# Attention scores two pairs ahead, zero matmuls at the changes of stage, and weight remainders split up, in a two-block network kernel

## The reference

```python
def sliding_window_attention(u, k, v, w_q, q_norm, sinks, rel_bias, w_o):
    q = rmsnorm((u @ w_q).reshape(...), q_norm)
    ...
    def block(args):                         # 128 queries against 256 keys
        s = einsum('bqkrd,bskd->bkrqs', qk, kk) * scale + bias
        s = where(valid, s, -inf)
        m = maximum(max(s), sink)
        p = exp(s - m)
        denom = sum(p) + exp(sink - m)
        return einsum('bkrqs,bskd->bqkrd', p / denom, vk)
    ...
    return o @ w_o
```

## Time and profile before

| | |
|---|---|
| median of 3 runs | 2444.01 us (2443.07 to 2445.93) |
| the profiled execution | 2443.57 us, its span 2441.5 us |
| mean granted clock of PE | 0.964 of full speed |
| busy: PE | 2213.6 us (91%) |
| busy: DVE, ACT | 1517.4 us (62%), 1005.7 us (41%) |
| weight transfers | 354.88 MB on SP's queue, 44.1% of 16 engines |

### The profile page before, as it was taken

The page is one execution under the profiler, slowest core; times in us unless marked ns, Lnnn a source line. Parts: engine busy times, 40 slices in busy tenths (PEclk is TensorE's granted clock), DMA queues, the critical chain, the costliest instruction groups (busy, mean ns, idle before and its releaser), DMA issues.

```text
span 2441.5 us, 43688 instructions
## 1 busy us (share of the span) xinstructions
PE 2213.6 (91%) x15328; PEld 1975.8 (81%) x15336; DVE 1517.4 (62%) x2937; ACT 1005.7 (41%) x1601; POOL 17.0 (1%) x23
## 2 busy tenths in 40 slices
PE   7998787999989987799898878997788999999998
PEld 6998786799979975699887647886766999999997
DVE  4555776655545544555575556888966666666665
ACT  4344453533443444533452244224533444444443
POOL 0000000000000000000000000000000000000000
PEclk9999898999989999899999989998999999999999
DMA  5554342455465543355440013433355766666664
GB/s 190 181 188 165 133 143 70 145 193 191 167 224 180 188 132 101 112 188 190 147 147 29 11 43 129 145 113 109 130 166 180 235 204 204 219 187 189 188 188 132
DMA packets 106677, 376.95 MB, mean 154 GB/s; under 512 B 11552, under 2 KB 17456, under 8 KB 105840
## 3 DMA queue, kind: packets, MB, share of 16 engines
q1 hardware_dynamic: 102528, 354.88, 44.1%
q0 software_dynamic: 4080, 21.15, 2.7%
HBM read 362.29 MB, written 13.69 MB: 154 GB/s over the span
## 4 chain that ended last, share of the span: by engine, by line
PE 77%; DVE 9%; DMA 4%; ACT 4%; issue 3%; DVEq 2%; ACTq 1%; SPq 0%
PE bank L340 60%; PE bank L366 6%; PE bank L1325 3%; DVE w_lo L301 2%; DMA ring<-in_expert_v 2%; PE bank L2188 1%; DMA ring<-in_ssm_in 1%; ACT w_hi L296 1%; DVE arena L2389 1%; DMA ring<-in_expert_u 1%; PE bank L531 1%; PE bank L322 1%; PE bank L768 1%; ACT arena L1123 1%; PE bank L324 1%
## 5 line engine op out<-in xcount | busy, mean ns | idle before, releaser
L301 DVE TENSOR_TENSOR w_lo<-ring,w_hi 128x1024 fp32r<-128x1024 f32 x581 | 701.7, 1223 | 459.1 <-ACT w_hi L296 457.8
L296 ACT ACTIVATE w_hi<-ring 128x1024 fp32r<-128x1024 f32 x581 | 604.4, 1056 | 694.6 <-PE bank L340 540.9
L340 PE MATMUL bank<-u_hi,w_hi 128*128 128x256 f32 x2568 | 733.6, 286 | 10.9 <-DVE arena L861 7.7
L340 PE MATMUL bank<-u_lo,w_hi 128*128 128x256 f32 x2568 | 730.2, 284 | 0.0
L340 PE MATMUL bank<-u_hi,w_lo 128*128 128x256 f32 x2568 | 729.8, 284 | 0.0
L340 PEld LDWEIGHTS bank<-u_hi,w_hi 128*128 128x128 f32 x2568 | 496.2, 193 | 22.2 <-issue 10.4
L340 PEld LDWEIGHTS bank<-u_lo,w_hi 128*128 128x128 f32 x2568 | 496.3, 193 | 7.5 <-issue 0.5
L340 PEld LDWEIGHTS bank<-u_hi,w_lo 128*128 128x128 f32 x2568 | 495.8, 193 | 0.0
L340 PE MATMUL bank<-w_hi,x_hi 128*128 128x512 f32 x992 | 396.0, 399 | 21.0 <-DVE w_lo L301 14.8
L340 PE MATMUL bank<-w_lo,x_hi 128*128 128x512 f32 x992 | 392.8, 396 | 0.0
L340 PE MATMUL bank<-w_hi,x_lo 128*128 128x512 f32 x992 | 389.6, 393 | 0.0
(11 more groups left out here) (304 smaller groups left out, 1789.4 us busy)
## 6 DMA issues: line engine op xcount, KB each, us to landing
ring<-in_w SPq DMA_DIRECT2D x264, 512.0 KB, 3.6
ring<-in_expert_u SPq DMA_DIRECT2D x128, 512.0 KB, 3.6
ring<-in_expert_v SPq DMA_DIRECT2D x128, 512.0 KB, 4.3
ring<-in_ssm_in SPq DMA_DIRECT2D x40, 512.0 KB, 4.3
gate_dram<-con SPq DMA_DIRECT2D x16, 576.0 KB, 3.0
arena<-gate_dram POOLq DMA_DIRECT2D x9, 1024.0 KB, 8.7
ring<-in_ssm_out SPq DMA_DIRECT2D x16, 512.0 KB, 3.4
ring<-in_w_o SPq DMA_DIRECT2D x16, 512.0 KB, 4.2
```

The costliest lines, as they stand in the source:

```text
L296: act.activation(w_hi[slot][:, :], ring[slot][:, :], ACT.Copy).then_inc(hi_made[slot], 1)
L301: dve.tensor_tensor(w_lo[slot][:, :], ring[slot][:, :], w_hi[slot][:, :].bitcast(F32), ALU.subtract).then_inc(freed[slot], 1)
L340: mm = pe.matmul(out, left[a], right[b], start=start and n == 0, stop=stop and n == 2, skip_group_check=True)
```

## The change

Three edits.

1. **Attention.** The banks are dealt by use and no more by parity: `Q` (banks 0, 1), scores `SC` (2, 3), transposes `PT` (4, 5), outputs `OUT` (6). In step j PE does the transposes of pair j, the query sums of j+2, the outputs of j, the queries of j+3 and the scores of j+2. ACT does the copies of j, the root of j+2, the output copy of j, the exponentials of j+1 and the squares of j+3. DVE takes the maxima of j+1, makes the queries of j+2 and scales the probabilities of j+1. SP's queue is put in the matching order.
2. **Zero matmuls.** `norm_tensor` issues eight matmuls of zeros (bf16, 512 columns, into bank 4) ahead of its first wait and four more between its two halves, in all changes of stage but those at the start and behind kv: ssm, ffn1, kv, attn, ffn3, rwkv and peer, 84 matmuls in all.
3. **Remainders.** Of a stage's led tiles the first remainder is made where all were, the second between `update_h` and `norm_vector`, and the rest behind `norm_vector`.

```diff
-        def lead_vector(dve, before):
-            after = stages[stages.index(before) + 1:][:1] if before else stages[:1]
-            for slot, ring_stage in LEAD.get(after[0], ()) if after else ():
+        def lead_vector(dve, stage, some):
+            for slot, ring_stage in LEAD.get(stage, [])[some]:
                 make_lo(dve, slot, ring_stage, 0)
+
+        def lead_next(dve, before):
+            for stage in stages[stages.index(before) + 1:][:1]:
+                lead_vector(dve, stage, slice(0, 1))
...
-            lead_vector(dve, stage)
+            lead_next(dve, stage)
             update_h(dve, 0.5, upd[stage], stage)
...
+        def keep_busy(pe, n):
+            for _ in range(n):
+                pe.matmul(bank[4][:, :], zeros[:, 0:P], zeros[:, :], start=True, stop=True)
+
         def norm_tensor(pe, s):
+            calm = s == stages[0] or stages[stages.index(s) - 1] == "kv"
+            if not calm:
+                keep_busy(pe, 8)
             for q in range(4):
+                if q == 2 and not calm:
+                    keep_busy(pe, 4)
                 pe.wait_ge(S("norm_rows"), 4 * norm_no[s] + q + 1)
...
+            query(0, 0)
+            query(1, 0)
+            table(0, 0)
+            query(0, 1)
+            table(1, 0)
+            with sp.Fori(0, 2) as i:
+                query(1, i + 1)
+                table(0, i + 1)
+                query(0, i + 2)
+                table(1, i + 1)
+            query(1, 3)
+            table(0, 3)
+            table(1, 3)
...
-            def step(b, i):
-                nb, ni = 1 - b, i + b
-                queries(nb, ni)
+            def step(b, i, further=True, ahead=True):
                 turn(b, i)
-                query_sums(nb, ni)
+                if ahead:
+                    query_sums(b, i + 1)
                 outputs(b, i)
-                scores(nb, ni)
+                if further:
+                    queries(1 - b, i + 1 + b)
+                if ahead:
+                    scores(b, i + 1)
...
+            def step(b, i, further=True, ahead=True, more=True):
+                j1 = 2 * i + b + 1
                 for a in range(2):
                     act.wait_ge(S("p_turned"), 2 * j1 - 1 + a)
-                    act.activation(prob_t[:, b, a, :], bank[4 * b + a][:, 0:384], ACT.Copy).then_inc(S("p_turned_out"), 1)
+                    act.activation(prob_t[:, b, a, :], PT[a][:, 0:384], ACT.Copy).then_inc(S("p_turned_out"), 1)
+                if ahead:
+                    root(b, i + 1)
+                act.wait_ge(S("o_done"), j1)
+                act.activation(o_all[:, bass.ds(2 * i + b, 1), :], OUT[:, 0:T].unsqueeze(1),
+                               ACT.Copy).then_inc(S("o_ready"), 1)
                 if more:
-                    root(nb, ni)
+                    exps(1 - b, i + b)
+                if further:
+                    square(1 - b, i + 1 + b)
...
+            def step(b, i, ahead=True):
+                maxima(1 - b, i + b)
+                if ahead:
+                    query(b, i + 1)
+                normalise(1 - b, i + b)
...
                 if s in norm_no:
+                    if s != stages[0]:
+                        lead_vector(dve, s, slice(1, 2))
                     norm_vector(dve, s)
-                    if s == stages[0]:
-                        lead_vector(dve, None)
+                    lead_vector(dve, s, slice(0 if s == stages[0] else 2, None))
```

More of the change, by code:

```diff
@@ L1033, in attn_sync, with query @@
             sp.wait_ge(S("h_updated"), 4 * upd["attn"] + 1)
-            with sp.Fori(0, 4) as i:
-                for b in range(2):
-                    load(sp, b, io["w_q"][bass.ds(2 * i + b, 1), :, :], "attn", i)
-                    sp.wait_ge(S("scored"), 4 * i + 2 * b + 2)
-                    for a in range(2):
-                        table = bias_dram[bass.ds(4 * i + 2 * b + a, 1), 127:127 + P * 383].rearrange(
-                            "h (q y) -> q (h y)", y=383)
-                        sp.dma_start(bias_tile[:, b, a, 0:P], table[:, P:2 * P]).then_inc(S(f"bias_loaded{b}"), 16)
-                        sp.dma_start(bias_tile[:, b, a, P:384], table[:, 0:2 * P]).then_inc(S(f"bias_loaded{b}"), 16)
+            def query(b, i):
+                load(sp, b, io["w_q"][bass.ds(2 * i + b, 1), :, :], "attn", i)
@@ L1151, in query, with maxima @@
                 dve.wait_ge(S("qk_rooted"), 2 * i + b + 2)
-                dve.scalar_tensor_tensor(q_t[:, b, :], bank[4 * b][:, 0:T], V("q_norm"), at_root[:, b, :],
+                dve.scalar_tensor_tensor(q_t[:, b, :], Q[b][:, 0:T], V("q_norm"), at_root[:, b, :],
                                          ALU.mult, ALU.mult).then_inc(S("q_ready"), 1)
-            def step(b, i, more=True):
+            def maxima(b, i):
                 j1 = 2 * i + b + 1
@@ L1193, in attn_vector @@
                 step(1, i)
-            step(0, 3)
-            step(1, 3, more=False)
+            step(0, 3, ahead=False)
             out_vector(dve, "attn_out", o_all)
```

90 lines of the change are left out of this document (53 added, 37 removed).

## The result

| | before | after |
|---|---|---|
| median | 2443.54 us (4 runs, 2442.26 to 2445.93) | 2417.22 us (4 runs, 2411.58 to 2423.82) |
| ratio, 95% interval | | 0.9895 (0.9877 to 0.9912) |
| profiled execution, its span | 2443.57, 2441.5 us | 2418.02, 2416.0 us |
| mean granted clock | 0.964 | 0.968 |

The forecast was 2420 (2413 to 2429), faster: it held. The kernel is 1.05% faster. Note how far apart the four runs after lie, 12 us.

A forecast was written before the change was run, and what follows sets the result against it. No engine is full: PE waits in serial chains or runs at half clock. Attention -21.1, ffn3 -2.7, ffn1 -1.2, rwkv -1.1 and ssm +3.0 sum to -23.1, from 2443.57 to 2420.5, said as 2420 us; range 2413 to 2429.

The forecast's parts named there:

- The loop: Attention loop: seven steps take 47.0 us against 71.0, five of 6.8 and two of 6.5; -24.0 us.
- the rings: Attention step: the longer of two serial rings sets it, DVE and ACT at 6.5 us, PE at 6.8.
- low clock inside the loop: Attention loop: sign of failure, as are steps staying above 8 us; no size given.
- ffn3 and ffn1: Changes of stage into them: products start 1.1 us earlier; ffn3 -2.7 with 1.6 of low clock gone, ffn1 -1.2.
- The ssm stall: ffn0 to ssm: PE stands 3.5 us for the dt remainder, then half clock; +3.0 us, bounds +1.7 and +5.6.
- rwkv: ffn3 to rwkv: next tiles wait for loads, so only the earlier u_lo counts; -1.1 us.
- The zero matmuls: Changes of stage: covered by PE's waits, cost taken as 0; full clock kept, eight transposes 1.10 us instead of 1.97.
- zeros don't hold the clock: Rival, changes of stage: 0.44 lost at three of them and 1.6 us in ffn3; 2423.4 us, chance 0.08.
- The queue: Rival, attention: w_q loads stuck behind bias tables on SP's queue land late; slower, 2456 us, chance 0.03.
- Long steps: Rival, attention: further semaphore waits on PE and late maxima make steps of 8.5 us; 2433 us, chance 0.09.
- The cheap stall: Rival, ssm: stall costs +0 to +1.7 instead of +3.0, each attention step 6.5 us; 2417 us, chance 0.13.
- No difference: Rival, whole kernel: everything cancelled; chance 0.01.

The follow-up runs named there:

- Experiment 8: Kernel after with half of each query product left out in the attention loop; steps of 6.33 to 6.37 us from the second pair on, except the last (6.87).
- experiment 7: Kernel of experiment 6 with more zero matmuls in waits of ssm and attention and their output products; 2405.09 us, ratio 0.9853.
- experiment 2: Kernel after without its 84 zero matmuls; 2424.3 us, ratio 0.994.
- experiment 3: Kernel after with all led remainders made in a row ahead of the update of h, not split; 2418.06 us, ratio 0.9912.
- experiment 5: Kernel after run once more, unchanged; 2416.31 us (six runs, 2411.2 to 2423.1), ratio 0.9897.
- experiment 6: Kernel after with 36 + 4 zero matmuls at ffn2, 21 at rwkv, and ssm's dt remainder second on DVE alone; 2409.19 us, ratio 0.9867.
- experiment 4: Kernel after with ssm's dt tile second, its hi part and remainder made ahead of slot 1's; 2416.18 us, ratio 0.9894.
- experiment 9: Kernel after with w_q loads for pairs 3 to 7 held back until DVE has read the scores two pairs before; 2433.56 us, single run.
- experiment 1: Kernel after with the attention reordering alone, no zero matmuls and no split of the remainders; 2425.4 us, ratio 0.9933.

## Why the prediction was right

**The loop**, the largest term, was right to 0.2 us: 47.2 against 47.0, steps of 6.83 against 6.8 while there are queries. Experiment 8 shows the rings at 6.83 and 6.37 against 6.8 and 6.5. That the sum agrees so closely is in part luck: the two steps without queries were put at 6.5 each and took 6.15 and 6.82. The last one ran in part at half clock; at full clock it takes 6.26, and the loop 46.7 (experiment 7). I had named low clock inside the loop as a sign of failure, and it did turn up there (clock 0.85 over the last two steps), though it cost only this 0.6. The start came at +2.7 against +2.9. What I missed is the end: +1.2 from the last transposes to the end of the stage against "unchanged". There half clock came later than before and reached into the output product; with full clock throughout, in experiment 7, this part took 27.9, against 30.3 here and 29.1 before. So attention gave 19.9 and not 21.1.

**ffn3 and ffn1** gave 2.6 and 1.3 against 2.7 and 1.2. Experiments 2 and 3 part them: without the split 0.67 is lost in each, which is the wait of ACT for DVE; without the zeros 2.2 and 1.5.

**The ssm stall** was predicted as 3.5 us, with half clock behind it, and +3.0 at the row of line 333. Measured: 3.22, half clock, +3.1. At the next long wait of PE it is +2.6, and +4.0 in the mean of four executions, so that far the chain is serial as I said. The stage as a whole shows +0.5 in the pair of profiles, and +3.1 when the mean of four with this code is set against that of two with the code of before (experiment 5). That this is the forecast +3.0 is worth little, as single executions differ by 4. What removes the stall has ssm at 255.9 and 257.6 (experiments 3 and 6), but also at 264.6 (experiment 4).

**rwkv** was right in its size (1.6 against 1.1) by the wrong reason. I had u_lo 1.1 earlier. It is 0.14 earlier, seen from PE's end: 10.13 after it, against 10.27. The norm does begin earlier, its transposes 5.38 after PE's end against 6.04, which is the 0.67 of ACT. But the clock fell in the wait, so the four zeros between the halves took 1.91 in place of 1.03 and held up the second eight transposes. With 21 zeros ahead, in experiment 6, the first products begin 9.42 after PE's end, against 10.17 here and 10.32 before. The rows are PE's transposes with the zeros between them and the first matmuls of the branch, after; then the same transposes and matmuls before:

```profile
1190.85 1.36 PE L545 MATMUL bank<-con,arena 128*128 128x128 f32 x8 [3.64 <-DVE arena L496]
1192.01 1.91 PE L533 MATMUL bank<-zeros 128*128 128x512 bf16 x4
1193.71 1.64 PE L545 MATMUL bank<-con,arena 128*128 128x128 f32 x8
...
1214.64 4.92 PE L1339 MATMUL bank<-arena 64*128 64x256 f32 x16 [1.98 <-ACT arena L1558]
```

```profile
1215.72 1.97 PE L531 MATMUL bank<-con,arena 128*128 128x128 f32 x8 [6.04 <-DVE arena L492]
...
1239.10 3.85 PE L1283 MATMUL bank<-arena 64*128 64x256 f32 x16 [1.98 <-ACT arena L1502]
```

PE still idles 3.64 in front of the transposes, and the clock falls all the same (1.36 and 1.64 for eight, where 1.10 is full clock). The branch's first matmuls (line 1339, 1283 of before) begin 29.2 after PE's end in the one and 29.4 in the other (ends 1185.5 and 1209.7): of the 1.1 only 0.2 came. The rest of the stage's 1.6 lies later, and the same code gave 4.7 in experiment 5.

**The zero matmuls** are where the working was weakest. I counted them only where the clock fell in the profile of before, and set kv, ffn2, attn and peer to 0. The saving there is not seen in that one pair of profiles (kv 18.8 in both), but without them kv falls to half clock (21.2, 22.7). Their worth is 7 us by the medians and more by the ratios, not the 2.9 by which the rival "zeros don't hold the clock" was priced; its 2423.4 lies near the 2424.3 of experiment 2 only because my sum stood 3 us above the result. The Trainium skill (TensorE: Matmul & The Clock Gate, Part 1: The HAM clock gate), cited in the prediction, lets the point at which the clock changes differ from run to run. The runs agree as far as they go: in experiment 2 the change to kv and that to attn both have a gap of 1.72 us, and the clock fell in the first and held in the second. The page also ties the fall to a whole idle window; in kv the clock fell in two kernels with no single idle piece longer than 1.72 us.

**The sum.** -23.1 forecast, -25.5 in the profiled pair, and 2417.2 against 2420.5 by the median. The misses are the tail of attention (+1.2), ssm (-2.5), ffn0 (-0.9, nothing predicted) and rwkv (-0.5). The last three are of the size by which one code differs between executions, and the 3 us that I allowed for the clock should have been 6: the runs of the kernel after go from 2411 to 2424. The upper bound of 2429 also does not add up: its parts (steps of 7.6, the stall at +5.6) give 2427, and 2430 with the 3 us.

**The rivals.** The queue: excluded by the loop's rows, its mechanism shown by experiment 9. Long steps: excluded by 6.83. The cheap stall is the rival whose number, 2417, is the one measured, and the +0.5 of ssm in the profiled pair fits it. Its mechanism doesn't: the attention steps are 6.83 and not 6.5, the clock fell at the stall, and PE's long wait ends 2.6 to 5.0 later in four executions. Zeros that don't hold the clock: excluded by experiment 2. No difference: no.

## What to carry to other kernels

Where each step is a serial chain through three engines, list the rings (each engine's own work in a step, and the chain that returns to the same engine) and take the longest; it gave the new step to 0.05 us. Fill PE's idle pieces with matmuls on zeros only up to the wait that is there: eight matmuls of 1.90 us were free in gaps of 1.72 and 2.66 us, sixteen of 3.63 cost 1.0 to 1.9 us each time. A remainder or any other preparation that is put behind something must be one that is used late; look at the order of use, not at the order of slots.

## What the runs showed of the hardware

- A wait of 1.7 us between long runs of matmuls (ahead of kv) kept the full clock in the profile of before and lost it in those of experiments 1 and 2. Whether it falls can't be read from one profile.
- The time of one code goes with the clock, loosely. The first four runs of the kernel after have mean granted clocks of 0.972, 0.969, 0.968 and 0.967 at 2411.58, 2416.43, 2418.02 and 2423.82 us; but of the six of experiment 5 two at 0.970 are 7 us apart.
- Zero matmuls in bf16, which carry no data, hold the granted clock. Experiments 6 and 7 differ in them alone: 0.973 to 0.977 in the six runs of one, 0.978 to 0.980 in the six of the other.
- Half clock costs less than its length suggests. From the spans and clocks of the two profiled executions, the kernel of experiment 6 has 2 x (1 - 0.974) x 2406.7 = 125 us of it, that of experiment 7 has 2 x (1 - 0.980) x 2400.6 = 96 us. The difference of 29 us would be worth 15 if PE were busy all the time; the spans differ by 6.1, the medians by 4.1. PE waits for others in much of it, which is the likely reason. The Trainium skill (TensorE: Matmul & The Clock Gate, HAM oscillation — how this bites in real kernels) takes half of the throttled time as the penalty, which would be those 15 us; this pair shows less than half of that.
